# Expert weight chunks by column halves, loaded in two transfers and awaited half by half

## What is computed

```python
def _expert_choice_ffn(u, w_router, w_g, w_u, w_d):
    b, n, _ = u.shape
    cap = CAPACITY_FACTOR * n // N_EXPERTS          # 32 tokens for each of 16 experts
    logits = jnp.einsum('bnd,de->ben', u, w_router, preferred_element_type=jnp.float32)
    aff = jax.nn.softmax(logits, axis=1)
    gate, idx = lax.top_k(aff, cap)
    xe = u[bidx, idx]
    hg = jnp.einsum('becd,edf->becf', xe, w_g)
    hu = jnp.einsum('becd,edf->becf', xe, w_u)
    ye = jnp.einsum('becf,efd->becd', jax.nn.silu(hg) * hu, w_d) * gate[..., None].astype(u.dtype)
    return jnp.zeros_like(u).at[bidx, idx].add(ye)
```

## Time and profile before

| | us |
|---|---|
| median of three runs | 1992.25 (1987.91 to 1992.79) |
| the profiled execution | 1987.57 |
| its span, first to last instruction | 1985.7 |
| PE busy | 1650.3 (83%) |
| DVE busy | 571.8 (29%) |
| ACT busy | 335.8 (17%) |
| POOL busy | 142.9 (7%) |

### The profile page before, as it was taken

How to read it: one execution, slowest core, us unless ns; L and a number is a source line. 1 busy time by engine, 2 the same in 40 slices (tenths; PEclk the granted TensorE clock), 3 DMA queues, 4 the chain that set the end, 5 groups by cost and what they waited for, 6 DMA issues and landing times.

```text
span 1985.7 us, 25792 instructions
## 1 busy us (share of the span) xinstructions
PE 1650.3 (83%) x11442; PEld 941.7 (47%) x11442; DVE 571.8 (29%) x1063; ACT 335.8 (17%) x725; POOL 142.9 (7%) x137
## 2 busy tenths in 40 slices
PE   6998766656668998666667659999999999999999
PEld 3544121211116853211212128877578687775785
DVE  0564010101006741100001022542443525523434
ACT  1141100000000011000000002242332113433320
POOL 0000000000000000000000000220032102100221
PEclk9998987878769998878878679999999999999999
DMA  9999999999999979999999994122533341124320
GB/s 402 427 419 375 427 427 428 428 427 428 428 428 425 428 318 414 428 427 429 427 428 428 428 423 186 46 70 86 197 129 128 138 170 42 65 86 170 149 85 22
DMA packets 45293, 586.59 MB, mean 295 GB/s; under 512 B 5248, under 2 KB 5408, under 8 KB 9472
## 3 DMA queue, kind: packets, MB, share of 16 engines
q1 hardware_dynamic: 42624, 575.05, 69.9%
q0 software_dynamic: 2128, 8.46, 1.1%
q10 hardware_dynamic: 432, 1.44, 0.2%
HBM read 583.87 MB, written 1.06 MB: 295 GB/s over the span
## 4 chain that ended last, share of the span: by engine, by line
PE 58%; DMA 37%; DVE 3%; ACT 1%; issue 1%; SPq 0%; DVEq 0%; ACTq 0%
DMA arena<-in_experts 29%; PE ps L1284 16%; PE ps L1670 8%; DMA spare<-in_experts 7%; PE ps L1547 5%; PE ps L1693 4%; PE ps L1689 4%; PE ps L1452 3%; PE ps L2040 2%; DMA ring<-in_stream 1%; PE ps L1242 1%; PE ps L1791 1%; PE ps L1313 1%; PE ps L2070 1%; PE ps L1561 1%
## 5 line engine op out<-in xcount | busy, mean ns | idle before, releaser
L1547 PE MATMUL ps<-arena 128*32 128x512 f32 x1372 | 220.9, 769 | 122.8 <-DMA arena<-in_experts 121.3
L1547 PE MATMUL ps<-ring,arena 128*32 128x512 f32 x1312 | 200.4, 740 | 111.0 <-DMA ring<-in_experts 108.3
L1547 PEld LDWEIGHTS ps<-arena 128*32 128x32 f32 x1372 | 44.4, 125 | 264.5 <-DMA arena<-in_experts 142.6
L1284 PE MATMUL ps<-arena,ring 128*128 128x256 f32 (+1 forms) x880 | 168.2, 353 | 0.0
L1284 PEld LDWEIGHTS ps<-arena,ring 128*128 128x128 f32 x880 | 149.5, 191 | 17.8 <-issue 1.1
L1547 PEld LDWEIGHTS ps<-ring,arena 128*32 128x32 f32 x1312 | 40.8, 122 | 244.7 <-DMA ring<-in_experts 133.1
L1670 PE MATMUL ps<-arena,ring 128*128 128x256 f32 x640 | 154.9, 387 | 0.0
L1670 PEld LDWEIGHTS ps<-arena,ring 128*128 128x128 f32 x640 | 117.0, 190 | 23.8 <-issue 7.8
L2486 DVE TENSOR_TENSOR arena<-ps,gate 128x512 f32<-128x512 f32 x16 | 11.1, 692 | 287.4 <-PE ps L1547 287.4
L1547 PE MATMUL ps<-spare,arena 128*32 128x512 f32 x336 | 60.5, 855 | 34.7 <-DMA spare<-in_experts 33.9
L878 ACT ACTIVATE arena<-ps,modcol 128x128 f32<-128x128 f32 x32 | 14.6, 457 | 418.6 <-PE ps L1561 418.6
(11 more groups left out here) (445 smaller groups left out, 2222.7 us busy)
## 6 DMA issues: line engine op xcount, KB each, us to landing
arena<-in_experts SPq DMA_DIRECT2D x85, 2048.0 KB, 40.6
ring<-in_experts SPq DMA_DIRECT2D x82, 2048.0 KB, 40.7
ring<-in_stream SPq DMA_DIRECT2D x52, 2048.0 KB, 8.7
spare<-in_experts SPq DMA_DIRECT2D x21, 2048.0 KB, 40.5
arena<-in_stream SPq DMA_DIRECT2D x13, 2048.0 KB, 27.4
spare<-in_stream SPq DMA_DIRECT2D x10, 2048.0 KB, 9.2
arena<-in_stream SPq DMA_DIRECT2D x2, 1024.0 KB, 26.6
gate<-in_b_mod POOLq DMA_DIRECT2D x4, 512.0 KB, 10.8
```

What stands on the lines that cost most here:

```text
L1284: mm = M(dst, lhs(k), rhs(k), start=k == 0, stop=k == n - 1)
L1547: mm = M(bank(b + half)[32 * e:32 * e + 32], x[:, k, 32 * e:32 * e + 32], wk(e, half), start=k == 0, stop=k == KD - 1, tile_position=(0, 3 ...
```

## The change

In HBM the columns of a chunk's row are sorted anew: first columns 0 to 511 of all four experts, then columns 512 to 1023 of all four. The slices that TensorE reads are picked accordingly. Each of the 186 chunks of nine-room kind is loaded with two transfers of 1024 KB, with rows of 8 KB, the first half on the old semaphore and the second on a new one for each room (`second_landed`). The products of half 0 wait for the first, those of half 1 for the second. The chunks of the rooms WHOLE, HALVED and PIECED are loaded as before, with their new layout.

```diff
+        second_landed = [ctx.enter_context(nc.semaphore(f"second_half_landed{s}")) for s in range(WIDE)]
...
-                        sp.dma_start(room(n, EG * D), src).then_inc(landed[place[n]], 16)
+                        if place[n] != WHOLE:
+                            sp.dma_start(room(n, EG * D)[:, 0:2 * D], src[:, 0:2 * D]).then_inc(landed[place[n]], 16)
+                            sp.dma_start(room(n, EG * D)[:, 2 * D:], src[:, 2 * D:]).then_inc(second_landed[place[n]], 16)
+                        else:
+                            sp.dma_start(room(n, EG * D), src).then_inc(landed[place[n]], 16)
...
                     if place[i] == PIECED:
-                        return lambda e, f: piece_of(i, e * D + f * HALF)
+                        return lambda e, f: piece_of(i, f * 2 * D + e * HALF)
                     parts_of = halves_of(i) if place[i] == HALVED else (room(i, EG * D)[:, 0:2 * D], room(i, EG * D)[:, 2 * D:])
-                    return lambda e, f: parts_of[e // 2][:, e % 2 * D + f * HALF:e % 2 * D + (f + 1) * HALF]
-
-                def products(b, x, k, wk, signal=None):
+                    return lambda e, f: parts_of[f][:, e * HALF:(e + 1) * HALF]
+
+                def second_half(g, m, k):
+
+                    i = base + (3 * g + m) * KD + k
+                    if place[i] in (WHOLE, HALVED, PIECED):
+                        return None
+                    return second_landed[place[i]], 16 * sum(key[0] == "expert" and place[n] == place[i] for n, (key, _) in enumerate(order[:i + 1]))
+
+                def products(b, x, k, wk, signal=None, second=None):
                     for half in range(2):
+                        if second and half:
+                            pe.wait_ge(*second)
                         for e in range(EG):
...
-                        products(0, ff["xg"], k, streamed(g, 0, k)).then_inc(used, 1)
+                        products(0, ff["xg"], k, streamed(g, 0, k), None, second_half(g, 0, k)).then_inc(used, 1)
...
-    a["experts"] = a["experts"].reshape(2, NG, 3 * KD, P, EG * D)
+    a["experts"] = a["experts"].reshape(2, NG, 3 * KD, P, EG, 2, HALF).transpose(0, 1, 2, 3, 5, 4, 6).reshape(2, NG, 3 * KD, P, EG * D)
```

More of the change, by code:

```diff
@@ L1581, in ffn @@
                     for k in range(KD):
-                        products(2, ff["xg"], k, streamed(g, 1, k)).then_inc(used, 1)
+                        products(2, ff["xg"], k, streamed(g, 1, k), None, second_half(g, 1, k)).then_inc(used, 1)
                     for b in range(2):
@@ L1592, in ffn @@
                             pe.wait_ge(*Sax.turn(g, "ht", k // 4))
-                        mm = products(4, ff["ht"], k, streamed(g, 2, k), up("down") if k == KD - 1 else None)
+                        mm = products(4, ff["ht"], k, streamed(g, 2, k), up("down") if k == KD - 1 else None, second_half(g, 2, k))
                         mm.then_inc(used, 1)
```

## The result

| | before | changed | predicted |
|---|---|---|---|
| median | 1991.66 us (6 runs, 1986.66 to 1993.05) | 1999.30 us (6 runs, 1997.83 to 2000.87) | 2003 (1990 to 2014) |
| ratio | | 1.0048, 95% interval 1.0034 to 1.0062 | 1.0054 |
| profiled execution | 1987.57 us | 1997.83 us (+10.3) | +10.8 |

A forecast was written before the change was run, and what follows sets the result against it. Loads were taken to pace the expert stretches and TensorE the rest. Profiled 1987.57 - 2.6 + 13.4 = 1998.4 us; with the median 4.7 above the profiled run, 2003 us, range 1990 to 2014.

The forecast's parts named there:

- Load-paced: In the expert stretches loads set the pace, 428 GB/s at share 1.01; starting a half earlier brings nothing in the middle.
- Rival 2: Expert loop is one of latency, not a queue: faster by 18 us, 1971.7 us with the ends; chance 0.04.
- Rows of 8 KB: Ring chunks in the expert stretches: smaller packets cost 0.08 us a chunk, 2 x 84 chunks, +13.4 us.
- The row of 2 and 4 KB packets: Stretch 171.5 to 176.5 us, used as a price: 16.5 ns a packet, +0.15 us a chunk, +25 us.
- Rivals 1 and 3: Rival 1, and one that rows of 8 KB cost more than 0.1 us a chunk: 2014.6 us, chance 0.10.
- Rival 1: The packets' cost in the expert stretches is hidden, under 0.05 us a chunk: not slower; chance 0.15.
- the halves alone: Stretch 751.7 to 754.1 us at 427 GB/s, the packet cost's lower bound: 0.011 us a chunk, +1.9 us.
- The ends: Last chunk of each layer: half 0 runs earlier, saving 0.96 us in layer 0 and 1.6 in layer 1, -2.6 us.
- The added waits and issues: 186 more waits in PE's queue and 186 more transfers issued by SyncE: zero.
- The queue's limit: SyncE's queue holds about nine transfers; blocked issues cost zero, landing falls from 40.6 to about 22 to 25 us.
- Rival 4: A full queue has gaps: engines idle 0.1 us behind each blocked issue, +34 us, 2037 us; chance 0.05.
- The signs: Expert stretches: nine chunks in 44.8 us, 420 to 423 GB/s, layer ends some 6 and 11 us later, slow SyncE issues.

The follow-up runs named there:

- the kernel of 64 partitions: Against the changed kernel: each chunk in two transfers of 64 partitions, rows of 16 KB, one wait for both; median 2402.76 us beside 1991.64.
- the layout alone: Against the changed kernel: one transfer and one wait a chunk again, new order of columns kept; ratio 1.0005 to the kernel before, median 1991.67 us.
- the kernels with one transfer and with four: Against the changed kernel: each chunk in one transfer out of two blocks, rows of 8 KB, ratio 1.0065; or in four transfers, rows of 4 KB, 1.0174.
- the kernel with both waits ahead: Against the changed kernel: two transfers kept, but TensorE waits for both halves ahead of a chunk's first product; ratio 1.0033, then 1.0036.

## Why the prediction was right, point by point

- *Load-paced.* Right: share 1.01 before and after, and the time moved with GB/s alone. Rival 2 (latency) is out: a half earlier start of every chunk did nothing for the distance of chunks (44.73 us for nine; 44.72 where a whole chunk was awaited).
- *Rows of 8 KB*, taken at 0.08 us a chunk. Measured 0.074 between chunks (44.73 against 44.06 for nine). On the path: the last half of layer 0 starts its products at 608.15, the last chunk before at 602.56, +5.6; layer 1 starts 4.3 us later and its last half starts at 1182.41 and not 1171.73, +10.7, so 6.4 in that layer. 12.0 for both where 13.4 was forecast. These starts are of one profile each and carry its chance: in the second profile the last half of layer 0 starts at 610.36. The distance alone gives 168 x 0.074 = 12.4. The nearest row, the halved chunk of the kernel before, had shown 2.48 us for a megabyte; twice that is 4.96, and it was the right one to lean on, with some luck: its +0.065 us stood on landing times rounded to 0.1. The row of 2 and 4 KB packets gave 16.5 ns for a packet where the experiments have 9: too much. That stretch also had rows of 2 KB and moved 164 to 524 GB/s from slice to slice; which of the two made its packets dear isn't shown. What the 9 ns are made of isn't shown either. Rivals 1 and 3 are out. Rival 1, and with it the lower end of the range, leaned on the +1.9 us of the halves alone: 1987.57 - 2.6 + 1.9 + 4.7 = 1991.5 us for the median. The distance gave 12.4 us in place of the 1.9.
- *The ends*, taken at -2.6 us. In the profiled pair: from the start of the last products to the y products 1.88 and 3.21 us before (602.56 to 604.44, 1171.73 to 1174.94), 1.00 and 1.00 after, so -0.9 and -2.2, -3.1 in all. The y products of the kernel before:

```profile
604.44 3.70 PE L1606 MATMUL ps<-arena 128*128 128x512 f32 x8
...
1174.94 3.74 PE L1606 MATMUL ps<-arena 128*128 128x512 f32 x8
```

  Over all profiles a whole last chunk took 1.87 to 3.57 us there and a last half 0.99 to 1.86; which one came went with the granted clock at that moment: 1.88 us at 1.00 (602.6 to 604.4 us) and 3.21 at 0.56 (1171.75 to 1174.9 us) for the kernel before, 1.00 us at 1.00 and 1.84 at 0.52 for halves of the changed kernel in its second profile's two layers. The mechanism was right, the term a little small. In the second profile the ends gave 1.00 and 1.84, so -2.3: which way the term misses changes with the execution.
- *The added waits and issues* cost nothing: SyncE's waits for rooms fell from 708.0 us to 217 while most of its issues took 2.1 us where they had taken 0.33, and GB/s with one transfer a chunk is the same, 421 from 310 to 350 us.

```profile
SPq L732 <- PE ps L1561: 217.2, 128, 7.2
...
319.32 2.13 SPq L732 DMA_DIRECT2D ring<-in_experts  x1
321.49 2.14 SPq L733 DMA_DIRECT2D ring<-in_experts  x1
```

- *The queue's limit.* I had put it at about nine transfers and forecast 22 to 25 us to landing; 27.0 were measured. It isn't a number of transfers: with one transfer of 272 packets a chunk the time was 32.9 us, with 512 KB in 144 packets 15.0 (pages of these two kernels, in this order; then the kernel of 64 partitions).

```profile
arena<-in_experts SPq DMA_DIRECT2D x85, 2048.0 KB, 32.9
...
arena<-in_experts SPq DMA_DIRECT2D x334, 512.0 KB, 15.0
...
arena<-in_experts SPq DMA_DIRECT2D x166, 1024.0 KB, 44.3
```

  Rate by time by packets, over 16 engines: 421 GB/s x 27.0 us is 10.8 transfers of 1 MB with 144 packets, 98 for each engine; 6.6 transfers of 272 packets give 112; 11.7 of 144 give 105. So roughly 100 packets of an engine were under way in all three, an estimate. Before, 8.3 chunks had 75, and no issue was held. It isn't the whole rule: by the same sum the kernel of 64 partitions had 68 (44.3 us at 322 GB/s, 80 packets a transfer), and its issues were held too (four in a row took 12.4 us). The step was wrong in what it counted, and it carried no time. Rival 4 is out: issues blocked all the time with 421 GB/s at a share of 1.01.
- *The signs.* The distance (44.73 for 44.8), the 421 GB/s at 1.01 and the slow issues came as named. The y products of layer 0 came 4.7 us later and those of layer 1 8.5 later, where 6 and 11 had been named; in the second profile it was 6.9 and 11.4.
- *The sum.* 12.0 - 3.1 is 8.9 us, and the long row of L1284 begins 1202.65 - 1193.87 = 8.8 us later. Not all of that is the two terms: the shift of 4.7 us at the end of layer 0 had become 4.3 at the first products of layer 1, and 0.3 us came in behind layer 1. The profiled spans differ by 10.3. The missing 1.5 us lie near 1703 us, where the changed kernel's TensorE had its lower clock for 3.4 us: its window from 1702 to 1708 us shows a granted clock of 0.72, where the kernel before has 1.00 at the same place (1693 to 1699 us).

```profile
1702.00:1708.00 6.00, 6.00 (x36) 4.26 (x36) 1.54 (x3) 0.01 (x1) 0.00 (x0) 0.72 0.03 10
```

This fall of the clock comes right behind the last of the three pauses. The second profile of the changed kernel has both as well, and so have the layout alone and the kernels with one transfer and with four (0.72 in the 6 us behind the pause in each of them, 1.00 there in all the others); the kernel before and the one that splits the last chunk only have the pause without the fall, and the kernel with both waits ahead has neither. So it isn't a part of the change, and no profile has the fall without the pause.

So the forecast of +10.8 us met the profiled +10.3 partly by luck: a packet term 1.4 us too large and an end term 0.5 too small, against 1.5 us of clock. The forecast of 2003 us for the median was 3.7 too high for a further reason: it carried over that the median lay 4.7 us above the profiled run, and with the changed kernel it lay 1.5 above.

## What to carry to other kernels

In a stretch paced by loads, starting on a part of a tile as soon as it landed was worth nothing here until the last tile (nine chunks in 44.73 us with it, in 44.72 without), and each row that was cut into shorter packets cost all the time: 9 ns of an engine a packet, and of the load time 1.5% from 16 to 8 KB, 4.5% to 4 KB. Split the one tile behind which everything waits, and leave the others whole (ratios of 0.9985 and 0.9977 here). Before believing a ratio of 0.3%, look where in the trace the difference is: a pause somewhere else can be nearly as large: the three in the second block make 4.4 us, 0.2%.

## What the runs showed of the hardware beside that

- The cost of a packet: 9 ns of an engine for each row packet more, from rows of 16 KB down to 4 KB; none to be seen for the small ones under 512 B: with 131 of 259 gone the distance was 4.969 us beside 4.970. Carried on to no cost at all, 2 MB would take 4.82 us, 435 GB/s (an estimate from the three distances).
- A queue that in three kernels had some 98 to 112 packets under way for each DMA engine (the estimate above) and held the issuing engine, in the changed kernel for 2 to 6 us an issue, with the engines' share at 1.01 (1.03 with four transfers).
- Transfers of 64 partitions, back to back, moved 322 GB/s where transfers of 128 moved 428, at the same share of 1.01 and the same packet size.
- With waits by halves TensorE's granted clock was a little lower: 0.79 and 0.77 in the two expert windows (0.79 and 0.80 in the second profile) against 0.81 and 0.80 and 0.81 to 0.82 with both waits ahead, at the same products. The single figures nearly touch; PE's busy time is clearer, 286 to 293 us in the windows of four expert stretches, 273 before and 269 to 271 with both waits ahead. That cost nothing between chunks, which loads pace: 44.73 us for nine beside 44.72 with one transfer and a whole chunk awaited.
- Pauses of TensorE of 0.9 to 1.8 us in rows of small products, without a releaser, at the same few places of the program; which of them occur differs between kernels and, for one of them, between executions of one kernel (the changed one, and the one that splits the last chunk only).
